# GpSimd in place of VectorE for one multiply of the first attention, with a fourth probability buffer

## The reference, cut to what matters

```python
def dense_block_attention(q, k, v, sink=None):
    ...
    def one(qi):
        s = jnp.einsum('bqkgd,bskd->bkgqs', qi, k).astype(jnp.float32)
        p = softmax_with_sink(s, sink).astype(v.dtype)
        return jnp.einsum('bkgqs,bskd->bqkgd', p, v)
...
    attn = dense_block_attention(q, jnp.concatenate([kc, k], axis=1), jnp.concatenate([vc, v], axis=1))
    conv = conv_module(glu, dw_w, dw_b, cn_g, cn_b)
...
        out_c = jnp.concatenate([dense_block_attention(qc, kc, vc),
```

## Time and profile before

| | |
|---|---|
| median of three runs | 1193.26 us |
| span of the profiled execution, first to last instruction | 1190.9 us |
| TensorE busy | 1151.1 us, 97% |
| VectorE busy | 688.0 us, 58% |
| ScalarE busy | 490.6 us, 41% |
| GpSimd busy | 8.5 us, 1% |

### The profile page before, as it was taken

One profiled execution on the slowest core, in us unless ns is written; L12 is line 12 of the kernel. 1 busy time (PEld: TensorE's weight loads), 2 busy tenths in 40 slices (PEclk: granted clock), 3 DMA queues, 4 the chain that ended last, 5 costly groups with the idle time before them and its releaser, 6 DMA issues.

```text
span 1190.9 us, 17575 instructions
## 1 busy us (share of the span) xinstructions
PE 1151.1 (97%) x7174; PEld 930.1 (78%) x7174; DVE 688.0 (58%) x1156; ACT 490.6 (41%) x750; POOL 8.5 (1%) x16
## 2 busy tenths in 40 slices
PE   4999999999999999999999999999999999999998
PEld 3777766777588888888887767899565798998997
DVE  3499987854542333333223358887789645554455
ACT  4343235643443332222222333367268635443442
POOL 0100000000000000000000000000000000000000
PEclk9999999999999999999999999999999999999999
DMA  9745654025553213332223564244140157655551
GB/s 359 264 142 170 210 201 171 1 68 216 178 176 106 82 60 98 114 121 92 79 80 114 187 216 139 78 138 142 37 132 12 39 179 244 212 177 177 191 167 67
DMA packets 117838, 167.73 MB, mean 141 GB/s; under 512 B 4766, under 2 KB 102664, under 8 KB 113544
## 3 DMA queue, kind: packets, MB, share of 16 engines
q1 hardware_dynamic: 117334, 166.23, 41.9%
q10 hardware_dynamic: 433, 0.51, 0.1%
HBM read 164.37 MB, written 1.05 MB: 139 GB/s over the span
## 4 chain that ended last, share of the span: by engine, by line
PE 76%; DVE 18%; ACT 3%; issue 2%; DMA 1%; SPq 0%; ACTq 0%; DVEq 0%; POOL 0%
PE acc L2021 18%; PE acc L2022 18%; PE acc L2023 18%; DVE Y L1331 6%; DVE w_lo L617 2%; PE acc L2083 2%; PE acc L2085 1%; PE acc L2084 1%; PE pmod L1958 1%; PE p L2370 1%; PE p L2369 1%; PE p L2371 1%; PE p L1906 1%; DVE sm L1411 1%; DMA xin<-in_ctx 1%
## 5 line engine op out<-in xcount | busy, mean ns | idle before, releaser
L617 DVE TENSOR_TENSOR w_lo<-raw,w_hi 128x1024 fp32r<-128x1024 f32 x226 | 253.8, 1164 | 242.4 <-ACT w_hi L607 242.1
L607 ACT ACTIVATE w_hi<-raw 128x1024 fp32r<-128x1024 f32 (+1 forms) x228 | 216.9, 999 | 425.6 <-PE acc L2023 351.9
L2021 PE MATMUL acc<-Hhi,w_hi 128*128 128x512 f32 (+1 forms) x976 | 333.5, 342 | 6.1 <-POOL ptap L659 4.5
L2022 PE MATMUL acc<-Hlo,w_hi 128*128 128x512 f32 (+1 forms) x976 | 331.2, 339 | 0.0
L2023 PE MATMUL acc<-Hhi,w_lo 128*128 128x512 f32 (+1 forms) x976 | 331.2, 339 | 0.0
L2021 PEld LDWEIGHTS acc<-Hhi,w_hi 128*128 128x128 f32 x976 | 185.6, 190 | 31.7 <-issue 9.1
L2023 PEld LDWEIGHTS acc<-Hhi,w_lo 128*128 128x128 f32 x976 | 185.5, 190 | 20.3
L2022 PEld LDWEIGHTS acc<-Hlo,w_hi 128*128 128x128 f32 x976 | 185.6, 190 | 20.0
L2021 PE MATMUL acc<-hid_hi,w_hi 128*128 128x512 f32 x248 | 97.9, 395 | 0.1
L2022 PE MATMUL acc<-hid_lo,w_hi 128*128 128x512 f32 x248 | 96.6, 390 | 0.0
L2023 PE MATMUL acc<-hid_hi,w_lo 128*128 128x512 f32 x248 | 96.6, 389 | 0.0
(11 more groups left out here) (375 smaller groups left out, 1546.6 us busy)
## 6 DMA issues: line engine op xcount, KB each, us to landing
raw<-in_mod_w SPq DMA_DIRECT2D x48, 1024.0 KB, 5.2
raw<-in_ffn_w_in SPq DMA_DIRECT2D x44, 1024.0 KB, 5.1
raw<-in_od_w_in SPq DMA_DIRECT2D x15, 1024.0 KB, 5.3
raw<-in_ev_w_in SPq DMA_DIRECT2D x10, 1024.0 KB, 7.6
raw<-in_ffn_w_out SPq DMA_DIRECT2D x12, 768.0 KB, 4.5
raw<-in_od_w_out SPq DMA_DIRECT2D x8, 1024.0 KB, 5.4
raw<-in_ffn_w_out SPq DMA_DIRECT2D x8, 1024.0 KB, 5.1
raw<-in_ev_w_out SPq DMA_DIRECT2D x8, 768.0 KB, 6.4
```

Of the source, the lines that this page charges most:

```text
L607: nc.scalar.activation(w_hi[:, w % 2, c0:c1], raw[:, r % RAW_SLOTS, c0:c1], ACT.Copy)\
L617: nc.vector.tensor_tensor(w_lo[:, w % 2, c0:c1], raw[:, r % RAW_SLOTS, c0:c1], w_hi[:, w % 2, c0:c1].bitcast(F32), ALU.subtract).then_inc( ...
L2021: mm(outs[m], hi[:, j, cols], xh, start=(first and j == 0), stop=False)
L2022: mm(outs[m], hi[:, j, cols], xl, start=False, stop=False)
```

## The change

The multiply by the inverse sums moves from VectorE to GpSimd. VectorE's reciprocal now releases GpSimd (`inv_ready`), and GpSimd's multiply raises `p_norm`, for which TensorE's transposes wait as before. `prob` and `sm` have four buffers; the exponential of u waits for the transposes of u - 4 where it waited for those of u - 3. The branches for a sink, which this attention does not have, are dropped from the code. The attention of layer 1 is not touched.

```diff
-        sm, smC = view("sm", [3, 8], r_sm), view("smC", [3, 8, 2], r_sm)
+        sm, smC = view("sm", [4, 8], r_sm), view("smC", [3, 8, 2], r_sm)
...
-        prob = view("prob", [3, T], r_h)
-        probT = view("probT", [2, T], r_h + 6144)
+        prob = view("prob", [4, T], r_h)
+        probT = view("probT", [2, T], r_h + 8192)
...
+            for u in range(32):
+                pool.wait_ge(s("inv_ready"), u + 1)
+                p_ = prob[:, u % 4, (0 if u % 4 < 2 else LAT):T]
+                nc.gpsimd.tensor_scalar(p_, p_, sm[:, u % 4, 4:5], None, ALU.mult).then_inc(s("p_norm"), 1)
+
             pool.wait_ge(s("h_lo"), 3 * KD)
...
-                    if u >= 3:
-                        act.wait_ge(s("pT_done"), n - 2)
+                    if u >= 4:
+                        act.wait_ge(s("pT_done"), n - 3)
...
                     if u is not None:
                         dve.wait_ge(s("exp_done"), n0 + u + 1)
...
-                        inverse = step.mark(V_.reciprocal(sm[:, u % 3, 4:5], total))
+                        V_.reciprocal(sm[:, u % 4, 4:5], sm[:, u % 4, 2:3]).then_inc(s("inv_ready"), 1)
...
-                    if u is not None:
-                        step.need(inverse)
-                        p_ = pr[:, u % 3, nk_of(u)[0] * P:T]
-                        V_.tensor_scalar(p_, p_, sm[:, u % 3, 4:5], None, ALU.mult).then_inc(s("p_norm"), 1)
```

More of the change, by code:

```diff
@@ L234, in build_trunk @@
         Y = view("Y", [BT, T], r_big + 20 * T * 4)
-        prob = view("prob", [3, T], r_h)
-        probT = view("probT", [2, T], r_h + 6144)
[L237 to L241, removed]
+        prob = view("prob", [4, T], r_h)
+        probT = view("probT", [2, T], r_h + 8192)
+        yc = view("yc", [BT, T], r_h + 12288)
+        yq = view("yq", [2, T], r_h + 20480)
+        l_rt = view("l_rt", [2, P], r_h + 24576)
+        l_mu = view("l_mu", [P], r_h + 25600)
+        yz = view("yz", [2, T], r_h + 26624)
         qrow = view("qrow", [P], r_big)
@@ L803, in exp @@
                     act.wait_ge(s("nb_ready"), n + 1)
-                    if u >= 3:
-                        act.wait_ge(s("pT_done"), n - 2)
+                    if u >= 4:
+                        act.wait_ge(s("pT_done"), n - 3)
                     c0, nkt = nk_of(u)
[L807 to L810, removed]
+                    A(pr[:, u % 4, c0 * P:T], sbank[u % 3][:, c0 * P:T], ACT.Exp, scale=qcol(u),
+                      bias=sm[:, u % 4, 1:2], accum_out=sm[:, u % 4, 2:3]).then_inc(s("exp_done"), 1)
                 exp(0)
@@ L1410, in softmax_step @@
                         dve.wait_ge(s("s_done"), n0 + v + 1)
-                        top = step.mark(V_.reduce_max(sm[:, v % 3, 0:1], sbank[v % 3][:, nk_of(v)[0] * P:T], AX.X))
+                        top = step.mark(V_.reduce_max(sm[:, v % 4, 0:1], sbank[v % 3][:, nk_of(v)[0] * P:T], AX.X))
                     if u is not None:
                         dve.wait_ge(s("exp_done"), n0 + u + 1)
[L1414 to L1422, removed]
-                    if u is not None:
-                        if sink is not None:
-                            step.need(summed)
-                        inverse = step.mark(V_.reciprocal(sm[:, u % 3, 4:5], total))
+                        V_.reciprocal(sm[:, u % 4, 4:5], sm[:, u % 4, 2:3]).then_inc(s("inv_ready"), 1)
                     if v is not None:
                         step.need(top)
[L1429 to L1434, removed]
-                        step.need(inverse)
-                        p_ = pr[:, u % 3, nk_of(u)[0] * P:T]
-                        V_.tensor_scalar(p_, p_, sm[:, u % 3, 4:5], None, ALU.mult).then_inc(s("p_norm"), 1)
+                        V_.tensor_scalar(sm[:, v % 4, 1:2], sm[:, v % 4, 0:1], qcol(v), -1.0, ALU.mult, ALU.mult)\
+                            .then_inc(s("nb_ready"), 1)
                 def out_lo(tile):
@@ L2234, in turn @@
                     for j in range(nkt):
-                        ins = T_(acc[:, 2 + u % 2, j * P:(j + 1) * P], pr[:, u % 3, (c0 + j) * P:(c0 + j + 1) * P])
+                        ins = T_(acc[:, 2 + u % 2, j * P:(j + 1) * P], pr[:, u % 4, (c0 + j) * P:(c0 + j + 1) * P])
                     ins.then_inc(s("pT_done"), 1)
```

## The result

The changed kernel takes 1203.13 us (median of four runs, 1201.16 to 1205.37) against 1193.40 us for the kernel before (now the median of four runs; the 1193.26 above is that of the first three): a ratio of 1.008, 95% interval 1.0067 to 1.0093. It is slower by 9.7 us; the forecast was 1195.1, with a range from 1192.2 to 1199.0.

A forecast was written before the change was run, and what follows sets the result against it. TensorE, busy 97% of the span, was taken to bound the kernel, VectorE the full regime. Two thirds of +0.7 us (tap first) plus one third of +4.1 (GpSimd first) gave +1.8: 1195.1 us, range 1192.2 to 1199.0.

The forecast's parts named there:

- GpSimd's price: GpSimd's multiply in the first attention: 0.75 us for 512 columns and 0.42 for 256, a pair 1.17, ends 0.84 and 1.99.
- one stream to read, so cheaper than two: GpSimd's one-input multiply lies between clearing (0.53 us for 512 columns) and two-input subtraction (1.29), nearer to the clearing.
- The loop: Tap-first case, steps with taps: loop through all engines, two units long, 7.70 us for four units against 7.44.
- the third stretch: 203.81 to 226.13 us, 12 units with a tap each, VectorE always busy: +0.8 us if the tap starts first.
- GpSimd waits for the tap: Steps with taps: the tap, with two SBUF inputs, keeps GpSimd out; its multiply runs only 0.84 us after the reciprocal started.
- nearly a tie: After the reciprocal GpSimd starts at 0.21 us, the tap at 0.25; tap first +0.7 us, GpSimd first +4.1, weighted two to one.
- Rival 1: Steps 8 to 25: GpSimd takes the port first in most steps and holds VectorE's tap; +4.1 us, 1197.4; chance 0.24.
- The first regime: 169.24 to 191.23 us, TensorE always busy: the multiply's loop, 6.44 us for four units, stays hidden behind 11.16.
- The sum, term by term: Tap first, within the attention: -0.4 us before the full regime, +0.8 in it, +0.3 at the ends, total +0.7.
- Rival 2: GpSimd multiplies at its subtraction's pace, 1.29 and 0.70 us: +5 us tap first, +12 GpSimd first; chance 0.08.
- the fourth buffer: ScalarE's exponentials in the attention: the relaxed wait on transposes frees nobody, worth nothing.
- the small ceiling of the offload: TensorE's own 7.2 us bound four units, so a lighter VectorE gains 0.25 there, at most 2.0 us in all.

The follow-up runs named there:

- run 11: Changed kernel with GpSimd's multiply written as a product of two inputs, the second the inverse sum repeated over the columns: 1198.30 us, ratio 1.0038.
- run 3: Changed kernel with 18 convolution taps left out and a one-input row maximum on VectorE in their place: 1201.38 us, ratio 1.006.
- run 4: Changed kernel with GpSimd multiplying only the first half of each unit's columns, the other half left out: 1195.78 us, ratio 1.0019.
- run 5: Changed kernel with its 18 taps moved to steps 0 to 8, two a step: 1201.66 us, ratio 1.0068.
- run 6: Kernel before, multiply still on VectorE, with its 18 taps moved to steps 0 to 8, two a step: 1191.97 us, ratio 0.9986.
- run 12: Changed kernel with GpSimd multiplying by the constant 0.5 in place of the inverse sums, normalization left out: 1201.09 us, ratio 1.0061.
- run 7: Changed kernel with a one-column clearing on VectorE before each tap in steps 8 to 25, so GpSimd starts first: 1202.62 us, ratio 1.0069.
- run 1: Changed kernel with the multiply back on VectorE and four buffers kept: 1192.92 us, ratio 0.9997.
- run 2: Kernel before with only the multiply moved to GpSimd, three buffers kept: 1202.53 us, ratio 1.0077.
- run 10: Changed kernel with GpSimd multiplying units 1 to 7 and, from 8 on, only units of 256 columns, VectorE the rest: 1195.64 us, ratio 1.0018.

## Why the prediction was wrong

*The step that failed is GpSimd's price.* I took 0.75 and 0.42 us and gave 1.29 and 0.70 as the upper ends, by the two-input subtraction. It is 1.56 and 0.92: above both ends. From the two sizes it is (1.56 - 0.92)/256 = 2.5 ns a column and 0.28 us fixed. The argument "one stream to read, so cheaper than two" was the fault: run 11 shows that the two-input form of the same multiply, with a repeated column as its second input, costs 1.04. The bound was not one, because the row was of another instruction and the order between the two was only reasoned. The Trainium skill, "GPSIMD Engine Reference", section Engine selection, has one-input operations at roughly line-rate and two-input ones slower; here the one-input multiply is 1.5 times the two-input one, so the measurement differs from the page.

*The loop was not the longest.* I closed the loop after two units, with two multiplies: 4.73 us and the rest. With the measured 0.78 us ahead of the multiply, 0.05 behind it and a pair of 2.48, that loop gives 4.73 + 2 x 0.83 + 2.48 = 8.87, near the measured 8.98 by luck of the sizes. The loop that binds holds three units of TensorE's order and one multiply: 5.96 + 0.63 + 0.25 + 2.10 + 0.04 = 8.98. Runs 3, 4, 5 and 6 follow it (8.44, 8.11, 8.43, 7.13). An estimate for my own 0.75 us goes from run 4, 8.11 us at 0.93: 8.11 - 0.18 = 7.93, not 7.70. By this estimate the third stretch would have grown by 3 x 0.49 = 1.5 and not 0.8 us even if the price had been right.

*The port, point by point.* That GpSimd waits for the tap was right (0.53 us; 0.59 forecast). That nearly a tie decides between two orders was right too, and the tap won in every step of the changed kernel without a small operation ahead of it: GpSimd starts 0.25 us after the reciprocal, not 0.21. Runs 11 and 12, with 0.22 and 0.24 us, have the other order. Rival 1's mechanism exists (run 11), but not as a whole instruction: GpSimd keeps VectorE out for 0.49 us of a 1.56 us multiply (run 7), for 0.41 of 1.49 in run 12, and for 0.85 of 1.04 in the two-input form. The Trainium skill, "SBUF — State Buffer", section Who interferes with whom, has it last for the whole instruction; run 7 shows a third.

*The first regime* was right but for its start. The chain of waits of the changed kernel, the pair that answers to the earlier trace rows:

```profile
173.19 1.00 PE pmod L1939 x8
...
184.35 1.00 PE pmod L1939 x8
```

It is 11.16 us for four units again, so even a multiply of 1.56 us, above the upper end up to which the prediction had it hidden, is hidden there. Not hidden is the multiply of unit 0: only one modulation product lies ahead of its transposes. The prediction's working treated the regime as a loop and did not look at its first turn. It cost 0.65 us and, in some executions, the clock.

*The sum, term by term:* forecast 0 in the first stretch, measured +0.65; -0.4 and +1.16 in the second; +0.8 and +4.63 in the third; +0.3 and +2.12 in the last. Rival 2, GpSimd at the pace of its subtraction, was priced at +5 to +12 and had a chance of 0.08. It is the case that came, with a still longer multiply: its order of size was right, its weight wrong, and its working, too, closed the loop after two units.

*Right without a reserve:* the fourth buffer (runs 1 and 2), the small ceiling of the offload (at most 2.0 us in the prediction; run 6, which takes load off VectorE without adding latency, gains 1.7), and that nothing behind the attention moves (-0.2 us).

## What to carry to other kernels

A busy engine is worth relieving only by what the next loop leaves: find it first, by following one tile through all engines and closing the loop after one, two and three units, since each closes with another share of the slow hand-over. The order of the operations on one engine belongs to the loop too (runs 7, 10 and 12). Here 0.3 us of VectorE's time per unit was exchanged for over 1 us of latency in a loop that had 0.3 us to spare for four units.

Work that can be moved in time within its own engine (the taps, to where TensorE is the bound) is better moved so than to a slower engine: it costs no hand-over.

A bound taken from a row of another instruction needs a reason that the rows themselves show. Where none does, the range has to be as wide as the engine's worst row and more.

## What the runs showed of the hardware

- GpSimd multiplying 128 partitions in place by a scalar of each partition: 1.56 us for 512 columns, 0.92 for 256, 0.60 for 128; by a constant 1.49 and 0.85; as a product with a repeated column 1.04 and 0.61. VectorE: 0.48 and 0.34.
- Beside the tap, a VectorE operation with two SBUF inputs that starts at the same time, GpSimd's multiply takes 0.53 us longer; beside a row maximum of one SBUF input (run 3) or a copy from PSUM of 512 columns (changed kernel, 193.68 us) it does not.
- GpSimd starting first holds the tap back until 0.49 us after its own start in the scalar form (512 columns, run 7), 0.41 us with a constant (run 12), and 0.85 us in the two-input form of 1.04 us (run 11); its own time stays.
- TensorE's granted clock fell to 0.50 (1.2 GHz) for some 3 us in five of the six profiles in which its first transposes waited for a GpSimd multiply of 1.49 or 1.56 us (the sixth is that of the changed kernel), and in none of the eight others, run 4 (0.93 us) and run 11 (1.04 us) among them.
